# A hybrid recurrent backbone: the modulation product in four column groups, and its weight slots at other places

## The chip, the cores and the metric

The kernel runs on one core of one Trainium2 chip. It is one program with five instruction streams: TensorE (matrix products, PE in the profile), VectorE (DVE), ScalarE (ACT), GpSimd (POOL) and SyncE (SP), which issues the loads of the weights. The metric is the device time of one execution in microseconds, here the median of three.

## The reference

Two layers over 512 positions (256 of context, 256 of latents) with 1024 features. Each layer takes a modulation vector of 6 x 1024 numbers for the context and one for the latents, from a product of SiLU of a condition vector with the matrix ada_w:

```
h   = adaLN(RMSNorm(x))          shift and scale from SiLU(c) (latents) and SiLU(c_ctx) (context)
P   = h W_in
Y_1 = RWKV-7 mixing, Y_2 = retention, Y_3 = HGRN2
x  += gate1 * ( sum_b sigmoid(P_gate_b) * (Y_b W_branch_b) ) W_out
x  += gate2 * SquaredReLU-MLP(adaLN(RMSNorm(x)))
'ada_w': (L, D, 6 * D) = (2, 1024, 6144),  'ada_b': (2, 6144)
```

For the change only the first line matters: 6144 columns for each of two layers, each a sum over 1024 rows, for two condition vectors, so a product with a left side of two columns. Shift and scale of the first norm are needed at the start of a layer, gate1 and the second norm's pair before the output projection and the MLP, gate2 in the MLP.

## The kernel before

All data lie transposed, features on the 128 partitions. The weights come from memory in slots of up to 2.3 MB into a ring of three places (RING = 3). The list of slots (schedule_slots) is also the order in which TensorE uses them. SyncE walks this list: the load of slot i waits until the last product that reads slot i - 3 is finished, since both have the same place in the ring. So three slots at most are in the chip at one time, and a slot that is put into the list takes a place of the ring from those around it.

The matrix ada_w is cut into 24 slots of 512 columns (12 for each layer), called (l, a). ADA_AT says at which place of the program each is used; a function modulation(place) stands at these places in the streams of TensorE, ScalarE and VectorE. For a slot TensorE makes eight products (L435), one for each 128 rows, with a stationary part of two columns, and adds them in one bank of PSUM, on two partitions. Each fp32 product is two instructions in the trace. ScalarE copies the two rows to work (L1455). Later TensorE turns the rows of an earlier slot into columns with four small products (L445), and VectorE adds the bias (L983). The program calls the four small products "ada columns".

Around these places TensorE runs strictly in the order in which the program is written, and so does each other engine. The stages of a layer: a norm (L416 sums squares, ScalarE makes the scaled tiles at L1439, and the first projections wait for them tile by tile), retention (ret_order, four heads), three small projections and then four heads of RWKV-7 (c = 0 to 3; L379 projects, then a long chain of 64x64 products from L401 on), HGRN2 (L736), the gated merge, the output projection (L805), a second norm and the MLP. Place names: "start", "norm1", "strips" (retention), "small" (after the small projections), "kk" and "keys" (in head c of RWKV-7, after its three projections), "out" (end of HGRN2), "norm2", "mlp".

The MLP of layer 0 has 16 slots of weights, mlp_slots. For each slot, a stage, TensorE makes 4 groups of 24 products (L826 to L828 or L840 to L842). Here fp32 values are split in a high and a low part: during stage n ScalarE makes the high part of the weights of slot n + 1 (weights_high, L1402, two halves) and VectorE subtracts it (weights_low, L942, two halves). On VectorE this stands ahead of the four drains of stage n (L1357 or L898):

```
for n, (kind, _, a) in enumerate(mlp_slots(l) ...):
    if n < 15:
        weights_low(l, n + 1)
    for j in range(4):
        ... drain group j of stage n ...
    if n == 1:
        modulation("mlp", l)
```

The results of TensorE's groups go to two banks (big), so group 2 of a stage can only start when VectorE has drained group 0.

## Time and profile before

| | |
|---|---|
| Median of three runs | 2955.51 us (2950.54 to 2956.82) |
| Profiled execution, its span | 2950.0 us |
| PE busy | 2763.4 us (94%) |
| PEld, weight loads of TensorE, beside PE | 1959.7 us (66%) |
| DVE, ACT, POOL busy | 977.6, 659.3, 449.8 us |
| L435, modulation products | 169.5 us busy, 384 instructions |
| L445, rows to columns | 24.0 us busy, 192 instructions |
| Moved by DMA | 239.42 MB, 81 GB/s on average |

The span goes from the first to the last instruction of one profiled execution; its own time is known as this span, and it lies at the low end of the three runs. A row of the timeline has start, duration, engine, line, operation, tiles, count, and in brackets how long the engine was idle before it and what ended that. TensorE is busy nearly all the time, but that says nothing on whether a given piece of its work could be left out without a wait of the same size in its place.

### The profile page before, as it was taken

What the parts mean: (1) busy time and instruction counts of PE and PEld (TensorE: products, weight loads), DVE (VectorE), ACT (ScalarE), POOL (GpSimd) and SP (SyncE); (2) the same over time, 40 slices, a digit from 0 to 9 for tenths busy, and PEclk for the clock granted to TensorE, in tenths of its full rate; (3) what the DMA queues carried; (4) which work ended last, traced back from release to release, by engine and by line L of the source; (5) the groups of instructions that cost most, each with busy time, mean ns of one, the idle gap of its engine ahead of it and who ended that gap; (6) DMA issues with size and microseconds to landing.
All of it is one profiled execution on the core that took longest, in us unless ns stands there. A gap on an engine that the chain in (4) does not pass through costs nothing. (4 is left out here: it accounts for less than half of the span.)

```text
span 2950.0 us, 51713 instructions
## 1 busy us (share of the span) xinstructions
PE 2763.4 (94%) x22928; PEld 1959.7 (66%) x22928; DVE 977.6 (33%) x1594; ACT 659.3 (22%) x923; POOL 449.8 (15%) x567
## 2 busy tenths in 40 slices
PE   8999999999999899999999999999888998799998
PEld 2553847658449656646888757386685657688887
DVE  1323443544116422225444332345444215211000
ACT  3213122331120311122222241323323120301100
POOL 0002221312006400000000000313223107100100
PEclk9999999999996799999999999999998996899999
DMA  7312220201110012232222251201000030143441
GB/s 300 139 50 77 78 80 3 80 5 57 49 70 33 33 64 97 73 126 87 86 101 99 86 194 72 95 25 52 19 14 30 2 121 33 61 157 115 160 154 72
DMA packets 18222, 239.42 MB, mean 81 GB/s; under 512 B 2001, under 2 KB 3153, under 8 KB 3409
## 3 DMA queue, kind: packets, MB, share of 16 engines
q1 hardware_dynamic: 16128, 218.11, 19.7%
q10 hardware_dynamic: 1872, 18.02, 1.5%
q8 instruction: 181, 2.97, 0.4%
q14 instruction: 41, 0.33, 0.0%
HBM read 230.88 MB, written 5.24 MB: 80 GB/s over the span
## 5 line engine op out<-in xcount | busy, mean ns | idle before, releaser
L379 PE MATMUL psum<-normed,weight_ring 128*128 128x256 f32 (+1 forms) x2320 | 771.6, 492 | 32.5 <-DVE work L892 11.5
L379 PEld LDWEIGHTS psum<-normed,weight_ring 128*128 128x128 f32 x2320 | 449.3, 195 | 342.8 <-issue 274.5
L392 PE MATMUL psum<-work 64*64 64x64 f32 (+1 forms) x9088 | 307.7, 222 | 13.9 <-ACT work L1614 10.5
L392 PEld LDWEIGHTS psum<-work 64*64 64x64 f32 x9088 | 294.9, 135 | 25.4 <-issue 14.5
L435 PE MATMUL psum<-weight_ring,derived 128*2 128x512 f32 x384 | 169.5, 602 | 12.4 <-ACT derived L1460 9.6
L898 DVE SCALAR_TENSOR_TENSOR work<-psum,derived,work 128x256 f32<-128x256 f32 x96 | 46.4, 484 | 394.7 <-PE psum L859 218.7
L736 PE MATMUL psum<-work 128*128 128x64 f32 x672 | 139.6, 399 | 13.9 <-DVE work L1277 10.8
L736 PEld LDWEIGHTS psum<-work 128*128 128x128 f32 x672 | 135.3, 310 | 18.0 <-DVE work L1277 12.3
L1204 DVE TENSOR_TENSOR work<-work,psum 128x512 f32<-128x512 f32 x144 | 99.0, 688 | 142.0 <-PE psum L392 141.9
L1778 POOL TENSOR_TENSOR work<-work,constants 128x512 f32<-128x512 f32 x80 | 108.2, 1352 | 205.8 <-DVE work L1187 140.6
L794 PE MATMUL psum<-work,weight_ring 128*128 128x512 f32 (+1 forms) x384 | 131.6, 485 | 0.0
L1801 POOL TENSOR_TENSOR work<-work 128x256 f32<-128x256 f32 x128 | 90.9, 710 | 260.7 <-PE psum L736 251.9
L435 PEld LDWEIGHTS psum<-weight_ring,derived 128*2 128x2 f32 x384 | 30.7, 85 | 141.2 <-issue 127.7
L1722 POOL TENSOR_TENSOR work<-work 128x512 f32<-128x512 f32 (+1 forms) x8 | 6.6, 826 | 746.7 <-DVE work L1069 746.7
L1323 DVE TENSOR_TENSOR work<-psum,work 128x512 f32<-128x512 f32 (+1 forms) x48 | 26.8, 558 | 274.4 <-PE psum L794 229.0
L859 PE MATMUL psum<-work,weight_ring 128*128 128x256 f32 x512 | 111.5, 379 | 0.0
L826 PE MATMUL psum<-normed_high,weights_high 128*128 128x512 f32 x256 | 104.5, 408 | 6.2 <-DVE work L1357 4.4
L859 PEld LDWEIGHTS psum<-work,weight_ring 128*128 128x128 f32 x512 | 97.3, 190 | 13.2
L828 PE MATMUL psum<-normed_high,weight_ring_parts 128*128 128x512 f32 x256 | 103.3, 404 | 0.0
L827 PE MATMUL psum<-normed_low_part,weights_high 128*128 128x512 f32 x256 | 102.8, 402 | 0.0
L840 PE MATMUL psum<-hidden_high,weights_high 128*128 128x512 f32 x256 | 101.8, 398 | 0.0
L842 PE MATMUL psum<-hidden_high,weight_ring_parts 128*128 128x512 f32 x256 | 101.7, 397 | 0.0
(229 smaller groups left out, 3929.8 us busy)
## 6 DMA issues: line engine op xcount, KB each, us to landing
weight_ring<-in_weights SPq DMA_DIRECT2D x78, 2048.0 KB, 7.9
weight_ring<-in_weights SPq DMA_DIRECT2D x16, 2304.0 KB, 8.6
weight_ring<-in_weights SPq DMA_DIRECT2D x10, 1536.0 KB, 6.6
x_scratch<-work ACTq DMA_DIRECT2D x2, 2048.0 KB, 11.5
work<-x_scratch ACTq DMA_DIRECT2D x2, 2048.0 KB, 9.0
work<-in_ret_constants ACTq DMA_DIRECT2D x2, 1152.0 KB, 14.5
work<-in_small_weights ACTq DMA_DIRECT2D x2, 1152.0 KB, 5.2
work<-in_x ACTq DMA_DIRECT2D x1, 2048.0 KB, 26.1
```

The lines of the kernel that those rows point to most:

```text
L379: last = mm(ps[:, 0:t1 - t0], tiled(s, j, k), hT[:, k, t0:t1], start=(k == 0), stop=(k == KT - 1))
L392: last = mm(ps[q, w * m:w * m + w], lhs(q, m), rhs(q, m), start=True, stop=True)
L435: last = mm(ps[rows_at(what), :], der[:, D_CS + 2 * k:D_CS + 2 * k + 2], s[:, BW * k:BW * k + BW], start=(k == 0), stop=(k == KT - 1))
L736: last = mm(cols(ps), k_[dd][:, t], cols(q_[dd]), start=True, stop=True)
L794: last = mm(ps[:, 0:t1 - t0], s[:, w0:w0 + P], work[:, Y[b] + 512 * k + t0:Y[b] + 512 * k + t1], start=(k == 0), stop=(k == NT - 1))
L826: mm(ps, w_hi, hi, start=(k == 0), stop=False)
L827: mm(ps, w_hi, hT_r[:, k, :], start=False, stop=False)
L828: last = mm(ps, s[:, P * t:P * t + P], hi, start=False, stop=(k == KT - 1))
L840: mm(ps, w_hi, hi, start=(k == 0), stop=False)
L842: last = mm(ps, s[:, P * t:P * t + P], hi, start=False, stop=(k == KT - 1))
L859: last = mm(ps[:, 0:t1 - t0], s[:, P * k:P * k + P], work[:, hid(k) + t0:hid(k) + t1], start=(k == 0), stop=(k == 31))
L1778: tt(chunks(B + (KTI if j % 2 else BT)), chunks(B + LT), over_chunks(kcol(K_LEV + 64 * j, 64), 64), ALU.mult).then_inc(pool_rwkv.sem, pool ...
```

## The change

Each slot's eight products now go to four column groups of TensorE's array in turn: the stationary part is 32 columns wide (two of them the condition, the rest zeros, in a new tile cond), and product k writes partitions 32 (k mod 4) to 32 (k mod 4) + 31. ScalarE copies all 128 rows. The four small products then use a matrix of two columns, K_SEL, which adds the four partial sums as they turn rows into columns. There is now one place in work for the rows instead of two, so "ada columns" of a slot follows directly after the products of the next slot, and ScalarE's copy waits for it.

The 24 slots move. Before, the slots of layer 1 were spread over RWKV-7 of layer 0, the end of HGRN2, the norms, and layer 1. Now layer 0's twelve stand at start, strips, small and RWKV-7 of layer 0; ten of layer 1's stand in the MLP of layer 0, one after each of the stages n = 1 to 10; two stand in norm1 and strips of layer 1. None is left at norm1 of layer 0, out, norm2, and small and RWKV-7 of layer 1. The masks of the scan also lose their second half (K_SCAN), the reversed one being equal to the first.

```
@@ -103,13 +104,14 @@
 
 ADA_AT = {
-    ("start", 0): [(0, 0), (0, 1), (0, 2), (0, 3), None], ("norm1", 0): [(0, 4), (0, 5)], ("strips", 0): [(0, 6)],
-    ("small", 0): [(0, 7)],
-    ("kk", 0, 0): [(0, 8)], ("keys", 0, 0): [(1, 0)], ("kk", 0, 1): [(0, 9)], ("keys", 0, 1): [(1, 1)],
-    ("kk", 0, 2): [(0, 10)], ("keys", 0, 2): [(1, 2)], ("kk", 0, 3): [(1, 3)],
-    ("out", 0): [(0, 11)], ("norm2", 0): [(1, 4)], ("mlp", 0): [(1, 5)],
-    ("norm1", 1): [(1, 6), (1, 7)], ("strips", 1): [(1, 8)], ("small", 1): [(1, 9)],
-    ("kk", 1, 0): [(1, 10)], ("kk", 1, 1): [(1, 11)], ("kk", 1, 2): [None],
+    ("start", 0): [(0, 0), (0, 1), (0, 2), (0, 3), None], ("strips", 0): [(0, 4)],
+    ("small", 0): [(0, 5)],
+    ("kk", 0, 0): [(0, 6)], ("keys", 0, 0): [(0, 7)], ("kk", 0, 1): [(0, 8)], ("keys", 0, 1): [(0, 9)],
+    ("kk", 0, 2): [(0, 10)], ("keys", 0, 2): [(0, 11)], ("kk", 0, 3): [None],
+    ("mlp", 0, 1): [(1, 0)], ("mlp", 0, 2): [(1, 1)], ("mlp", 0, 3): [(1, 2)], ("mlp", 0, 4): [(1, 3)],
+    ("mlp", 0, 5): [(1, 4)], ("mlp", 0, 6): [(1, 5)], ("mlp", 0, 7): [(1, 6)], ("mlp", 0, 8): [(1, 7)],
+    ("mlp", 0, 9): [(1, 8)], ("mlp", 0, 10): [(1, 9)], ("mlp", 0, 11): [None],
+    ("norm1", 1): [(1, 10)], ("strips", 1): [(1, 11), None],
 }
 
@@ -149,8 +151,7 @@
         if l < L - 1:
             for n, key in enumerate(mlp_slots(l)):
                 out += [(key, 4 * KT * P)]
-                if n == 1:
-                    ada("mlp", l)
+                ada("mlp", l, n)
         else:
             out += [(("m1", l, a), 4 * KT * P) for a in range(8)]
             out += [(("m2", l, f), 32 * P) for f in range(8)]
@@
+        cond = sb("condition_columns", [P, KT * 32])
@@ -332,14 +334,7 @@
             if what is None:
                 return [rows.pop(0) for _ in range(len(rows))]
             rows.append(what)
-            return [rows.pop(0)] if len(rows) > 2 else []
-
-        ada_order = [what for place in ADA_AT.values() for what in place if what is not None]
-
-        def rows_at(what):
-
-            p0 = 32 + 32 * (ada_order.index(what) % 2)
-            return slice(p0, p0 + 2)
+            return [rows.pop(0)] if len(rows) > 1 else []
 
         ret_order = [("P", 0), ("R", 0), ("P", 1), ("A", 0), ("R", 1), ("O", 0), ("P", 2), ("A", 1), ("N", 0), ("R", 2),
@@ -432,18 +427,17 @@
                         ps = mid.fill("ada", *what)
                         eng.wait_ge(*mid.freed())
                         for k in range(KT):
-                            last = mm(ps[rows_at(what), :], der[:, D_CS + 2 * k:D_CS + 2 * k + 2], s[:, BW * k:BW * k + BW],
-                                      start=(k == 0), stop=(k == KT - 1))
+                            g = 32 * (k % 4)
+                            last = mm(ps[g:g + 32, :], cond[:, 32 * k:32 * k + 32], s[:, BW * k:BW * k + BW],
+                                      start=(k < 4), stop=(k >= 4))
                         last.then_inc(mid_filled.sem, mid_filled.step(("ada", *what)))
                     for before in finished:
-                        q = rows_at(before)
                         eng.wait_ge(loaded_constants.sem, loaded_constants.at("constants"))
                         eng.wait_ge(act_cond.sem, act_cond.at("drained", "ada", *before))
                         ps = outb.fill("ada columns", *before)
                         eng.wait_ge(*outb.freed())
                         for j in range(4):
-                            last = mm(ps[:, 2 * j:2 * j + 2], work[q, ROWS2 + P * j:ROWS2 + P * j + P],
-                                      kc[q, K_ID + q.start:K_ID + q.stop], start=True, stop=True)
+                            last = mm(ps[:, 2 * j:2 * j + 2], wk(ROWS2 + P * j, P), kcol(K_SEL, 2), start=True, stop=True)
                         last.then_inc(out_filled.sem, out_filled.step(("ada columns", *before)))
             eng.wait_ge(loaded_vectors.sem, loaded_vectors.at("vectors"))
@@
-                    if n == 1:
-                        modulation("mlp", l)
+                    modulation("mlp", l, n)
@@
+            nc.vector.memset(cond[:, :], 0.0).then_inc(vec_cond.sem, vec_cond.step(("columns clear",)))
+            eng.wait_ge(vec_cond.sem, vec_cond.n)
@@
-                        G, sg, msk = wk(RW_D[d] + LT), wk(RW_D[d] + WW), kcol(K_SCAN + 512 * d, N)
+                        G, sg, msk = wk(RW_D[d] + LT), wk(RW_D[d] + WW), kcol(K_SCAN, N)
-                            G, sg, msk = G[:, ::-1], sg[:, ::-1], msk[:, ::-1]
+                            G, sg = G[:, ::-1], sg[:, ::-1]
@@ -1447,17 +1441,18 @@
                 for what in ADA_AT.get(place, ()):
                     if what is not None:
-                        q = rows_at(what)
                         eng.wait_ge(mid_filled.sem, mid_filled.at("ada", *what))
-                        if len(rows) > 1:
-                            eng.wait_ge(out_filled.sem, out_filled.at("ada columns", *rows[-2]))
+                        if rows:
+                            eng.wait_ge(out_filled.sem, out_filled.at("ada columns", *rows[-1]))
                         rows.append(what)
-                        act(work[q, ROWS2:ROWS2 + BW], mid.get("ada", *what)[q, :], ACT.Copy).then_inc(
+                        act(wk(ROWS2), mid.get("ada", *what), ACT.Copy).then_inc(
                             act_cond.sem, act_cond.step(("drained", "ada", *what)))
                         eng.wait_ge(act_cond.sem, act_cond.n)
             eng.wait_ge(loaded_vectors.sem, loaded_vectors.at("vectors"))
-            act(dcol(D_CS, 16), par[:, L * NPL + 8:L * NPL + 24], ACT.Silu).then_inc(act_cond.sem, act_cond.step(("cond silu",)))
+            eng.wait_ge(vec_cond.sem, vec_cond.at("columns clear"))
+            act(cond.rearrange("p (k m) -> p k m", m=32)[:, :, 0:2],
+                par[:, L * NPL + 8:L * NPL + 24].rearrange("p (k s) -> p k s", s=2), ACT.Silu).then_inc(act_cond.sem, act_cond.step(("cond silu",)))
             eng.wait_ge(act_cond.sem, act_cond.n)
             eng.wait_ge(vec_cond.sem, vec_cond.at("lb centred"))
             act(dcol(D_TMP + 8, 16), dcol(D_TMP + 8, 16), ACT.Exp).then_inc(act_cond.sem, act_cond.step(("lb exp",)))
@@
-    k[:, K_SCAN:K_SCAN + N], k[:, K_SCAN + N:K_SCAN + 2 * N] = t % C != 0, t % C != C - 1
+    k[:, K_SCAN:K_SCAN + N] = t % C != 0
+    k[:, K_SEL], k[:, K_SEL + 1] = p % 32 == 0, p % 32 == 1

```

At two places TensorE's order shows the move. The first is the MLP of layer 0 behind its stages 1 and 2; weights_high_0 and _1 are the high parts of the slots, L826 to L828 and L840 to L842 are L820 to L822 and L834 to L836 of the changed kernel. Before:

```order
1480 L828 MATMUL psum<-normed_high,weight_ring_parts 128x512
1481 L435 MATMUL psum<-weight_ring,derived 2x512 x8
1482 L445 MATMUL psum<-constants,work 128x2 x4
1483 L840 MATMUL psum<-hidden_high,weights_high_0_58 128x512
...
1578 L842 MATMUL psum<-hidden_high,weight_ring_parts 128x512
1579 L840 MATMUL psum<-hidden_high,weights_high_0_60 128x512
```

The same places in the changed kernel:

```order
1474 L822 MATMUL psum<-normed_high,weight_ring_parts 128x512
1475 L431 MATMUL psum<-weight_ring,condition_columns 32x512 x8
1476 L834 MATMUL psum<-hidden_high,weights_high_0_58 128x512
...
1571 L836 MATMUL psum<-hidden_high,weight_ring_parts 128x512
1572 L431 MATMUL psum<-weight_ring,condition_columns 32x512 x8
1573 L440 MATMUL psum<-constants,work 128x2 x4
1574 L834 MATMUL psum<-hidden_high,weights_high_0_60 128x512
```

Before, one slot's products stood behind stage 1 and none between stage 2 and stage 3; now there is one behind each of stages 1 to 10, and with it one slot in the ring between each two MLP slots.

The second is the end of that MLP and the start of layer 1: the last sums of squares, the first projections (L379, now L374) and the products of the values (L474, now L468). Before:

```order
2832 L416 MATMUL psum<-work,constants 128x512 x3
2833 L435 MATMUL psum<-weight_ring,derived 2x512 x8
2834 L445 MATMUL psum<-constants,work 128x2 x4
2835 L435 MATMUL psum<-weight_ring,derived 2x512 x8
2836 L445 MATMUL psum<-constants,work 128x2 x4
2837 L379 MATMUL psum<-normed,weight_ring 128x256 x8
2838 L379 MATMUL psum<-normed,weight_ring 128x512 x8
2839 L435 MATMUL psum<-weight_ring,derived 2x512 x8
2840 L445 MATMUL psum<-constants,work 128x2 x4
2841 L474 MATMUL psum<-weight_ring,normed 128x128 x32
```

And in the changed kernel:

```order
2844 L411 MATMUL psum<-work,constants 128x512 x3
2845 L431 MATMUL psum<-weight_ring,condition_columns 32x512 x8
2846 L374 MATMUL psum<-normed,weight_ring 128x256 x8
2847 L374 MATMUL psum<-normed,weight_ring 128x512 x8
2848 L431 MATMUL psum<-weight_ring,condition_columns 32x512 x8
2849 L440 MATMUL psum<-constants,work 128x2 x8
2850 L468 MATMUL psum<-weight_ring,normed 128x128 x32
```

One slot's products instead of two stand between the norm and the first projection that waits for it.

## Rows read from the trace of the kernel before

**Rows 1.** Groups by line and shape, TensorE: the modulation products.
```profile
L435 PE MATMUL psum<-weight_ring,derived 128*2 128x512 f32 x384 | 169.5, 602 | 12.4 <-ACT derived L1460 9.6 <-DMA weight_ring<-in_weights 2.8
```

**Rows 2.** Timeline of TensorE, RWKV-7 of layer 0, head 0: start, us, what.
```profile
285.88 7.13 PE L379 MATMUL psum<-normed,weight_ring 128*128 128x512 f32 x16 [0.57 <-ACT work L1526]
292.94 7.03 PE L435 MATMUL psum<-weight_ring,derived 128*2 128x512 f32 x16
299.90 1.05 PE L445 MATMUL psum<-constants,work 2*128 2x2 f32 x8
...
378.68 1.98 PE L385 MATMUL psum<-work,constants 128*128 128x512 f32 x4 [1.10 <-DVE work L1231]
```

**Rows 3.** Timeline of TensorE, products of two 64x64 quarters in turn.
```profile
432.08 1.96 PE L401 MATMUL psum<-work 64*64 64x128 f32 x32
```

**Rows 4.** Start of the program: a window (DMA share, GB/s last), TensorE's timeline.
```profile
10.00:28.00 18.00, 15.24 (x33) 2.72 (x32) 1.40 (x8) 2.86 (x5) 0.00 (x0) 0.98 1.01 430
...
27.61 8.53 PE L435 MATMUL psum<-weight_ring,derived 128*2 128x512 f32 x16 [2.76 <-DMA weight_ring<-in_weights]
...
46.81 9.21 PE L416 MATMUL psum<-work,constants 128*128 128x512 f32 x16
```

**Rows 5.** Timelines at the first norm of layers 0 and 1.
```profile
68.06 14.00 PE L379 MATMUL psum<-normed,weight_ring 128*128 128x512 f32 x32
...
60.93 10.10 ACT L1439 ACTIVATE normed<-work,derived 128x256 f32<-128x256 f32 x16 [0.91 <-DVE work L919]
...
1723.21 10.59 PE L379 MATMUL psum<-normed,weight_ring 128*128 128x256 f32 x32
...
1712.33 10.10 ACT L1439 ACTIVATE normed<-work,derived 128x256 f32<-128x256 f32 x16 [0.91 <-DVE work L919]
```

**Rows 6.** Timelines of layer 1, before and at its first RWKV-7 head.
```profile
1889.47 4.09 PE L536 MATMUL psum<-work 64*128 64x512 f32 x8
...
1879.00 0.42 ACT L1544 ACTIVATE work<-work 128x256 f32<-128x256 f32 x1
```

**Rows 7.** Timeline of TensorE, RWKV-7 of layer 0, head 3.
```profile
654.43 7.13 PE L379 MATMUL psum<-normed,weight_ring 128*128 128x512 f32 x16
...
677.27 3.68 PE L401 MATMUL psum<-work 64*64 64x128 f32 x32 [4.01 <-DVE work L1178]
...
744.58 1.98 PE L385 MATMUL psum<-work,constants 128*128 128x512 f32 x4 [1.09 <-DVE work L1231]
```

**Rows 8.** Timeline of TensorE, RWKV-7 of layer 1, heads 1 and 2.
```profile
2014.04 7.13 PE L379 MATMUL psum<-normed,weight_ring 128*128 128x512 f32 x16 [0.80 <-ACT work L1526]
...
2101.15 1.13 PE L385 MATMUL psum<-work,constants 128*128 128x256 f32 x4 [0.58 <-DVE work L1231]
...
2126.87 7.13 PE L379 MATMUL psum<-normed,weight_ring 128*128 128x512 f32 x16 [0.88 <-ACT work L1526]
...
2213.80 1.13 PE L385 MATMUL psum<-work,constants 128*128 128x256 f32 x4 [0.58 <-DVE work L1231]
```

**Rows 9.** Timeline of TensorE, end of HGRN2 and second norm of layer 0.
```profile
1021.76 0.70 PE L385 MATMUL psum<-work,constants 128*128 128x512 f32 x1 [1.63 <-POOL work L1814]
...
1322.52 0.47 PE L826 MATMUL psum<-normed_high,weights_high 128*128 128x512 f32 x1 [0.42 <-DVE normed_low_part L932]
```

**Rows 10.** Windows and timelines of the MLP of layer 0, stages 1 to 3.
```profile
1367.40:1381.00 13.60, 13.56 (x49) 10.62 (x50) 5.54 (x8) 1.89 (x3) 0.00 (x0) 0.83 0.00 0
1389.00:1411.20 22.20, 22.20 (x97) 18.04 (x98) 7.65 (x9) 4.44 (x3) 0.00 (x0) 1.00 0.23 90
...
L1842 SPq DMA_DIRECT2D weight_ring<-in_weights x5: 327/328/328, 1351.9 to 1433.5; - x5
...
1359.99 3.87 ACT L1402 ACTIVATE weights_high<-weight_ring 128x2048 fp32r<-128x2048 f32 x2 [5.87 <-DMA weight_ring<-in_weights]
...
1362.04 4.62 DVE L942 TENSOR_TENSOR weight_ring_parts<-weight_ring,weights_high 128x2048 fp32r<-128x2048 f32 x2 [7.13 <-ACT weights_high L1402]
...
1367.44 0.79 PE L826 MATMUL psum<-normed_high,weights_high 128*128 128x512 f32 x1 [4.44 <-DVE work L1357]
```

More of the change, by code:

```diff
@@ L53 @@
 K_SCAN = 2048
-K_EPS = 3072
-K_ID2 = 3076
-NCONST = 3140
+K_EPS = 2560
+K_ID2 = 2564
+K_SEL = 2628
+NCONST = 2630
 R_COS, R_SIN, R_LAG = 0, 512, 1024
@@ L67 @@
 NPAR = L * NPL + 8 + 16
-D_MOD, D_HMU, D_QMU, D_OMU, D_OMKA, D_WS1, D_WS2, D_LG, D_CS, D_LOW, D_OML = (
-    0, 96, 111, 126, 141, 145, 161, 177, 185, 201, 217)
-D_TMP = 233
-NDER = 265
+D_MOD, D_HMU, D_QMU, D_OMU, D_OMKA, D_WS1, D_WS2, D_LG, D_LOW, D_OML = (
+    0, 96, 111, 126, 141, 145, 161, 177, 185, 201)
+D_TMP = 217
+NDER = 249
 Y = [0, 2048, 4096]
@@ L1370, in _ @@
                                 vec_mlp.also(("drained", "m2", l, f))
-                    if n == 1:
-                        modulation("mlp", l)
+                    modulation("mlp", l, n)
                 for f in range(KT if l == L - 1 else 0):
@@ L1701, in _ @@
                         eng.wait_ge(act_mlp.sem, act_mlp.n)
-                    if n_ == 1:
-                        modulation("mlp", l)
+                    modulation("mlp", l, n_)
                 for f in range(32 if l == L - 1 else 0):
```

## The prediction, made blind

> **What bounds the kernel now.** I read the page's table of engines first: PE is busy 94% of the span, so the order of TensorE's work sets the time, and the reader is to see which pieces of that work hide a wait. Then the groups by line: L435 is 384 instructions for 24 slots, 16 a slot, 169.5 us in all, 7.06 us a slot [rows 1]; with the four small products a slot costs 7.03 + 1.05 less their overlap, 8.0 us [rows 2]. If all of it were bare TensorE time, the 24 slots would be 193 us. Then the timelines around each place, to see what comes behind the product, and last the MLP of layer 0, where the new slots go: which load does a VectorE instruction wait for, and who waits for VectorE.
>
> **T, the price of one slot's products.** The trace has no product in several column groups with all rows in use. The nearest row has two quarters of the array, in turn: 32 products of 128 columns in 1.96 us, of which some 0.2 is the last one's tail, so 0.055 us each [rows 3]. One such instruction by itself would take 7.03/16 x 128/512 = 0.11 us [rows 2]. So two run at once there, and I see no more than two in any row. Bounds: 7.0 us (nothing runs at once) and 7.0/4, with a tail 1.9 us. Each product is two instructions for one group, the second of which can't pass the first; if starts are in order, then in the row g0, g0, g1, g1, ... the second half of one group runs beside the first half of the next, and never more. That is 9 steps of 0.44 us for 16 instructions: T = 4.0 us. It is also what halving by rows 3 gives (3.5) with a step to begin and end. I take 4.0. With its small products a slot is then 5.0 us, against 8.0.
>
> The Trainium skill (TensorE: Matmul & The Clock Gate, Part 3: Packing small matmuls) states that matmuls start and end strictly in program order, and a measured 2.38x for three column tiles of 512 columns; by the latter the products would take 7.0/2.38 = 3.0 us or less, an estimate that lies between my T and the lower bound. No row here shows four column groups. The in-order rule is the one that speaks against the full factor of four, and rows 3 agree with it so far as they go.
>
> **The slots outside the MLP, place by place.**
> Start of layer 0: four slots. The DMA moves 430 GB/s from 10 to 28 us [rows 4], its most in the trace, so the third slot lands at 27.6 us whatever TensorE does; a slot of 2.1 MB is 4.9 us at that rate, so the fourth lands at 32.5. Third product: 5.4 us at the low clock that follows the wait (the row's 8.53 against 7.03 shows such a clock), to 33; small ones to 34; fourth to 38; its copy must now wait for the small products before it, so the last small ones end at 40.7. Before, the norm began at 46.8 [rows 4]: gain 6.
> First norm of both layers: two slots stood there. ScalarE's tiles take 10.10 us and end at 71.0 and 1722.4; the projections began at 68.1 and 1723.2 [rows 5]. TensorE will now wait for tiles and go by them: the first projection ends 3 and 3.7 us sooner. The wait lowers the clock for a few us, so I take 5 for both instead of 6.8.
> strips and small of layer 0: 8.0 becomes 5.0 each, gain 6 for both. strips of layer 1 also gets one more set of small products: gain 2. small of layer 1 goes: gain 8, since what comes behind it, L536 at 1889.5, needs ScalarE's result of 1879.4 and so has 10 us to spare [rows 6].
> RWKV-7 of layer 0: two slots in heads 0 to 2, one in head 3. From the third projection to the sums at the end head 0 takes 92.8 us [rows 2], head 3 with one slot less takes 90.2 [rows 7]: 8.0 us of products taken away give 2.65, the rest turns into the 4.0 us wait for VectorE at L1178 and a slower L401 behind it [rows 7]. Two slots at T = 4.0 make 10 us, near head 3's 8: gain 2.65 x 3 = 8. Head 3 loses its slot: gain 0, it waits already.
> RWKV-7 of layer 1: head 1 with a slot takes 87.1 us, head 2 with two sets of small products (2 us) 86.9 [rows 8]. The slots were cover for a wait: gain 0 for both.
> out: the sums behind it wait for POOL anyway [rows 9]: gain 1. norm2: the MLP's first product comes at 1322.5 and waits for the split of its input by VectorE [rows 9], not for the slot: gain 0, and 8 us of idle TensorE ahead of it, -1 for the clock.
> Clearing cond, the scan's mask and 128 rows instead of 2 in ScalarE's copy (the same 512 columns) cost nothing: VectorE clears while TensorE waits for its first data.
> Sum: 6 + 5 + 6 + 2 + 8 + 8 + 0 + 1 - 1 = 35 us gained. With T = 1.9: 9 + 5 + 10 + 4 + 8 + 8 + 0 + 1 - 1 = 44.
>
> **The MLP of layer 0.** A stage at full speed is 96 products in 22.2 us, 5.55 a group [rows 10]. Stage 1 shows what a slot in the ring does. The load of MLP slot 2 had to wait for the end of stage 0 and was issued at 1351.9 [rows 10]; ScalarE had it at 1360.0, 8.1 us later; VectorE could begin L942 after the first half, at 1362.0, needed 4.62, and only then drained group 0; TensorE, done with groups 0 and 1 at 1363.0, waited 4.4 us until 1367.4, then did the last two groups at granted clock 0.83 in 13.6 us instead of 11.1 [rows 10]. Behind VectorE's L942 stand all drains of the stage, behind these the banks, behind these TensorE. Stage 1 was 29 us instead of 22.2. Stage 2, with its load issued earlier, ran at 22.2 [rows 10].
> In the changed kernel this is the rule. MLP slot n + 1 takes the place of modulation slot n - 1, whose products end about 1 us before stage n; ahead of it on the queue stands modulation slot n, released at the end of stage n - 1, T earlier. Counted from the end of stage n - 1: the modulation slot lands at 8.0, the MLP slot 4.9 later, 12.9 (its own issue at T = 4.0 plus 8 is sooner, so the rate decides). Then as in stage 1: 2.0 for ScalarE's first half, 4.6 for L942, 0.7 for the drain: group 2 starts at 20.2. TensorE was ready at 4.0 + 1.05 + 11.1 = 16.1, so it waits 4.1 us. With 11.1 for two groups the period is 31.3 us, plus 2.5 where the clock falls as in stage 1; I take half of that: 32.5. This holds for n = 2 to 10, nine times: 9 x (32.5 - 22.2) = 93. Stage 11 adds one slot without a stall (5.0) and one set of small ones (1.05); before's slot in the MLP goes (-8.0). Sum: 91 us lost. Bounds: without any fall of the clock 80, with one each time 102. T hardly matters here, since the load sets the period.
>
> **The sum.** 91 - 35 = +56 us on a span of 2950.0. The median of the runs, 2955.5, lies 5.5 above this span; so 3012 us, slower by 1.9%.
>
> **Rivals.**
> All four groups at once: T = 1.9. The period in the MLP stays 32.5, stage 11 costs 3 us less: 89 - 44 = +45, 3001 us. For it: nothing in the change limits it to two. Against: rows 3.
> The groups don't run at once: T = 7.0. Then the MLP slot is issued at 7 and lands at 15, period 34.6, loss 112 + 1; outside the MLP only what stood free counts, 2 + 5 + 8 + 1 - 1 - 1 = 14: +99, 3055 us. For it: here all groups read the same rows, in rows 3 each quarter has its own.
> The loads come in time: the MLP slot lands by 8.8 us (16.1 less the 7.3 behind it), and stages stay at 22.2. Then the MLP costs 10 x 5.0 - 8.0 + 1.05 - 1.05 = 42, and 42 - 35 = +7, 2962 us; with T = 1.9 it would be 21 - 44 = -23. For it: the DMA is idle half of each stage. Against: stage 1, where even a single load came 4.4 us late.
> On the other side, faster: outside the MLP TensorE is the bound everywhere, as 94% says, and whatever leaves it comes off the time. Before, 23 slots at 8.0 stood outside, now 14 at 5.0: 184 - 70 = 114 us gained against 91, -23, 2932 us. It decides from 91 us of gain on, 2.6 times my sum. Against: rows 7 and 8, where 8 us less gave 2.65 and 0.2.
>
> **How the numbers follow.** Forecast 0.45, T = 1.9 0.24, no concurrency 0.12, loads in time 0.11, TensorE the bound 0.08. The forecast's own spread is the clock (+-11) and a few us for each place. The time is the forecast's, 3012. The range reaches down past the case of 3001 with no fall of the clock (2990) and part of the way to loads that land early, 2972, and up to half way to the case of 3055, 3040. A difference under 0.2% (6 us) can't be told from none. Slower by more: the first three cases and half of the fourth, 0.86. Within: 0.04. Faster: 0.10.
>
> **What would show it.** L431's 384 instructions: a slot in 4.0 us, or 1.9, or 7.0. In the MLP of layer 0 TensorE waits some 4 us for L1352's drain or the add behind weights_low in each of stages 2 to 10, weights_high waits for the DMA, and the stretch from the first MLP product to the first norm of layer 1 is some 90 us longer; if the waits are missing, the forecast is wrong. In RWKV-7 of layer 1 nothing gets shorter; in layer 0 heads 0 to 2 get shorter by some 3 us each, with a new wait for L1178. SyncE's queue in the MLP waits for L431.

## The result and the profile after: slower by 2.4%

The changed kernel takes 3021.66 us, median of four runs (3020.16 to 3026.92), against 2953.03 (2949.03 to 2956.82) for four runs of the kernel before: ratio 1.0241, interval 1.0224 to 1.0258. The profiled executions have spans of 3018.8 and 2950.0 us, so the account below is of +68.8 us. One execution of a later kernel, the spread places, was in a slower state (3159.8 us at a granted clock of 0.811, its other four at 0.933 to 0.938) and is left out of every number.

From the page of the changed kernel, first its table of engines, then three groups by line (busy us, mean ns | idle before, and on what):

```profile
PE 2691.1 (89%) x22928; PEld 1965.7 (65%) x22928; DVE 978.2 (32%) x1595; ACT 659.0 (22%) x923; POOL 449.3 (15%) x567
```

```profile
L431 PE MATMUL psum<-weight_ring,condition_columns 128*32 128x512 f32 x384 | 51.3, 656 | 18.5 <-ACT condition_columns L1454 9.5 <-DMA weight_ring<-in_weights 9.0
L440 PE MATMUL psum<-constants,work 128*128 128x2 f32 x192 | 26.4, 260 | 11.9 <-issue 11.9
...
L935 DVE TENSOR_TENSOR weight_ring_parts<-weight_ring,weights_high 128x2048 fp32r<-128x2048 f32 x32 | 73.4, 2292 | 130.8 <-ACT weights_high L1396 130.2
```

The products fell from 169.5 us of busy time [rows 1] to 51.3. PE is busy 72.3 us less than before, and the span is 68.8 us longer: TensorE idles 141 us more. In the trace of before VectorE's L942 (here L935) has 25.4 us of idle time ahead of it; now 130.8 stand there. The waits of TensorE (what it waited for: us in all, times, longest) say the same from its side:

```profile
PE psum L396 <- DVE work L1173: 49.5, 8, 8.7
PE psum L834 <- DVE work L891: 38.1, 6, 7.7
PE psum L820 <- DVE work L1352: 32.7, 5, 7.3
```

In the kernel before, RWKV-7 waited less, and the drains of the MLP made TensorE wait once, 4.4 us:

```profile
PE psum L401 <- DVE work L1178: 20.9, 5, 6.6
...
PE psum L826 <- DVE work L1357: 4.4, 1, 4.4
```

Eleven waits, 70.8 us, are now in the MLP of layer 0 (L834, L820), one in each of the stages 1 to 11. The first row is RWKV-7: 28.6 us more than before, as slots that were cover for it are gone or shorter: with slots of 7.05 us in the same places (the run of the places alone, below) it is 32.9 us in five waits, and heads 0 to 2 of layer 0, which keep two slots each, have none of them.

The timeline of TensorE from the start to the second projection (start, us, engine, line):

```profile
9.50 3.64 PE L431 MATMUL psum<-weight_ring,condition_columns 128*32 128x512 f32 x16 [9.50 <-ACT condition_columns L1454]
...
31.80 1.92 PE L431 MATMUL psum<-weight_ring,condition_columns 128*32 128x512 f32 x16
...
36.41 7.68 PE L411 MATMUL psum<-work,constants 128*128 128x512 f32 x16
50.38 16.79 PE L374 MATMUL psum<-normed,weight_ring 128*128 128x512 f32 x32 [6.29 <-ACT normed L1433]
67.10 1.93 PE L431 MATMUL psum<-weight_ring,condition_columns 128*32 128x512 f32 x16
```

A slot's 16 instructions take 1.92 us, and 3.64 behind a wait. The norm begins 10.4 us sooner than in [rows 4], and the first projection ends 15.0 us sooner than in [rows 5].

Now the MLP, TensorE from the slot behind stage 1 to that behind stage 10, and the chain on ScalarE and VectorE that it waits for:

```profile
1343.73 1.93 PE L431 MATMUL psum<-weight_ring,condition_columns 128*32 128x512 f32 x16
...
1377.94 1.92 PE L431 MATMUL psum<-weight_ring,condition_columns 128*32 128x512 f32 x16
...
1399.88 0.80 PE L834 MATMUL psum<-hidden_high,weights_high 128*128 128x512 f32 x1 [7.74 <-DVE work L891]
...
1412.86 1.92 PE L431 MATMUL psum<-weight_ring,condition_columns 128*32 128x512 f32 x16
...
1434.34 0.79 PE L820 MATMUL psum<-normed_high,weights_high 128*128 128x512 f32 x1 [7.32 <-DVE work L1352]
...
1447.14 1.92 PE L431 MATMUL psum<-weight_ring,condition_columns 128*32 128x512 f32 x16
...
1651.82 1.92 PE L431 MATMUL psum<-weight_ring,condition_columns 128*32 128x512 f32 x16
```

```profile
1392.13 3.85 ACT L1396 ACTIVATE weights_high<-weight_ring 128x2048 fp32r<-128x2048 f32 x2 [10.57 <-DMA weight_ring<-in_weights]
...
1394.17 4.62 DVE L935 TENSOR_TENSOR weight_ring_parts<-weight_ring,weights_high 128x2048 fp32r<-128x2048 f32 x2 [13.05 <-ACT weights_high L1396]
1398.82 2.04 DVE L891 SCALAR_TENSOR_TENSOR work<-psum,derived,work 128x256 f32<-128x256 f32 x4
```

The nine periods from the first of these rows to the last take 308.1 us, 34.2 each, where stage 2 of before took 22.2 [rows 10]; the two shown are 34.9 and 34.3. Counted from 1377.94: the load is there at 14.2, L935 starts at 16.2, TensorE goes on at 21.9, having been ready at 14.2 too. Behind the wait the granted clock is lower, as a window over the last two groups of a stage shows (us, busy of five engines, granted clock, DMA share, GB/s):

```profile
1364.30:1377.90 13.60, 13.59 (x48) 10.61 (x48) 1.93 (x4) 0.00 (x0) 0.00 (x0) 0.82 0.00 0
1399.90:1412.80 12.90, 12.90 (x48) 10.16 (x48) 1.90 (x4) 0.00 (x0) 0.00 (x0) 0.86 0.00 0
```

11.1 us of products take 13.6 and 12.9, as in stage 1 of before [rows 10].

### The profile page after: what moved, and what is told of

The parts are those of the page before. It is cut to its first block and busy times, and to the rows that moved or that the text cites. A ratio compares the mean times of both kernels' runs of the same rounds, so it can differ in the third digit from the quotient of the medians.

```text
span 3018.8 us, 51716 instructions
## 1 busy us (share of the span) xinstructions
PE 2691.1 (89%) x22928; PEld 1965.7 (65%) x22928; DVE 978.2 (32%) x1595; ACT 659.0 (22%) x923; POOL 449.3 (15%) x567
## 5 line engine op out<-in xcount | busy, mean ns | idle before, releaser
L374 PE MATMUL psum<-normed,weight_ring 128*128 128x256 f32 (+1 forms) x2320 | 783.1, 497 | 41.7 <-ACT normed L1433 15.7
L374 PEld LDWEIGHTS psum<-normed,weight_ring 128*128 128x128 f32 x2320 | 453.3, 197 | 361.6 <-issue 287.0
L387 PE MATMUL psum<-work 64*64 64x64 f32 (+1 forms) x9088 | 307.3, 223 | 12.5 <-ACT work L1609 10.2
L387 PEld LDWEIGHTS psum<-work 64*64 64x64 f32 x9088 | 294.3, 135 | 24.0 <-issue 12.4
L820 PE MATMUL psum<-normed_high,weights_high 128*128 128x512 f32 x256 | 108.4, 424 | 41.8 <-DVE work L1352 32.7
L834 PE MATMUL psum<-hidden_high,weights_high 128*128 128x512 f32 x256 | 108.2, 423 | 38.1 <-DVE work L891 38.1
L396 PE MATMUL psum<-work 64*64 64x128 f32 (+1 forms) x1024 | 73.3, 308 | 65.3 <-DVE work L1173 49.5
L1318 DVE TENSOR_TENSOR work<-psum,work 128x512 f32<-128x512 f32 (+1 forms) x48 | 26.8, 558 | 274.8 <-PE psum L788 228.8
L935 DVE TENSOR_TENSOR weight_ring_parts<-weight_ring,weights_high 128x2048 fp32r<-128x2048 f32 x32 | 73.4, 2292 | 130.8 <-ACT weights_high L1396 130.2
L396 PEld LDWEIGHTS psum<-work 64*64 64x64 f32 x1024 | 64.6, 167 | 70.7 <-DVE work L1173 50.6
L835 PE MATMUL psum<-hidden_low,weights_high 128*128 128x512 f32 x256 | 105.3, 411 | 0.0
## 6 DMA issues: line engine op xcount, KB each, us to landing
work<-in_x ACTq DMA_DIRECT2D x1, 2048.0 KB, 25.4
```

Of the source, the lines that this page charges most:

```text
L374: last = mm(ps[:, 0:t1 - t0], tiled(s, j, k), hT[:, k, t0:t1], start=(k == 0), stop=(k == KT - 1))
L387: last = mm(ps[q, w * m:w * m + w], lhs(q, m), rhs(q, m), start=True, stop=True)
L396: last = mm(ps[q, 128 * m:128 * m + n], lhs(q, m), work[q, B + KR + 128 * m:B + KR + 128 * m + n], start=True, stop=True)
L820: mm(ps, w_hi, hi, start=(k == 0), stop=False)
L834: mm(ps, w_hi, hi, start=(k == 0), stop=False)
L835: mm(ps, w_hi, hidden_lo[:, k, :], start=False, stop=False)
```

## Experiments

All ratios are to the kernel before, timed beside it on the same chip; the chips differ from one group of experiments to the next, so medians of different groups are compared only roughly.

**Does the order of the groups matter?** The products of a column group were put next to each other (0, 0, 32, 32, 64, ...) instead of in turn. If an instruction can start only when the one before it has, four instructions in a row for one group stand in the way of the next group.

```
-                            g = 32 * (k % 4)
+                            g = 32 * (k // 2)
-                                      start=(k < 4), stop=(k >= 4))
+                                      start=(k % 2 == 0), stop=(k % 2 == 1))
```

> The changed kernel, but two products in a row go to the same column group (0, 0, 1, 1, 2, 2, 3, 3) instead of 0, 1, 2, 3, 0, 1, 2, 3. Theory Q (each column group has its own order, and a later group passes an earlier one that waits): a slot's products still take 1.9 us and the time stays at 3022. Rival O (starts are in program order, and an instruction waits for its group's predecessor): 13 steps of 0.43, 5.7 us a slot, and 3035 to 3050 us.

Measured: 3018.51 us (3014.01 to 3027.87), ratio 1.0228 [1.0208, 1.0248], the same as the changed kernel. One slot in its timeline:

```profile
241.95 1.94 PE L431 MATMUL psum<-weight_ring,condition_columns 128*32 128x512 f32 x16
```

1.94 us against 1.92. The four groups run beside each other in either order, where starts in program order would have given 5.7 us, by the count in the expectation. So the in-order start that gave my T = 4.0 doesn't hold here; that each column group keeps an order of its own is what fits both times, but the trace doesn't name the group of an instruction. The Trainium skill (TensorE: Matmul & The Clock Gate, Part 3: Packing small matmuls) states that matmuls start and end strictly in program order; by it this kernel would have needed well over 1.94 us a slot, and this measurement does not agree with it for products in different column groups.

**The groups alone, and the places alone.** One kernel has the four groups, two row places in work, and the places of before; only the three slots from small of layer 1 on went to places just behind the first projections of the retention heads of layer 1. Its stationary part is 32 neighbouring columns of a narrower cond; thirty of them give sums that nobody reads. The other has the new places, with all products in one column group (g = 0, 32 rows copied).

```
+                            g = 32 * (k % 4)
+                            last = mm(ps[g:g + 32, :], cond[:, 2 * k:2 * k + 32], s[:, BW * k:BW * k + BW],
+                                      start=(k < 4), stop=(k >= 4))
...
-    ("norm1", 1): [(1, 6), (1, 7)], ("strips", 1): [(1, 8)], ("small", 1): [(1, 9)],
-    ("kk", 1, 0): [(1, 10)], ("kk", 1, 1): [(1, 11)], ("kk", 1, 2): [None],
+    ("norm1", 1): [(1, 6), (1, 7)], ("strips", 1): [(1, 8)], ("ret", 1, 1): [(1, 9)],
+    ("ret", 1, 2): [(1, 10)], ("ret", 1, 3): [(1, 11), None],
```

> The four column groups with the slots where they stood before (places of rows doubled so that two slots can stand in a row; the last three slots of layer 1, whose row space collides with other data now, stand behind the projections of retention heads 1 to 3 instead). Theory R (the move of ten slots into the MLP costs the time, since each takes a ring place and its MLP neighbour's load starts a stage late, and VectorE's split of the weights stands ahead of its drains): the MLP keeps one stall as before and the groups' gain shows: about 2914 us, 39 under the kernel before. Rival G (the grouped product itself slows what is around it): 2950 or more.

> The changed kernel's places, but all eight products of a slot in one column group, one after the other, 7.0 us a slot. Theory R: the stall in the MLP is set by the load, so the slower product adds only some 2 us to each of nine stages, about 10 at the start and 15 to 20 elsewhere: about 3070 us. Rival P (TensorE's own time is what counts everywhere): 24 x 5.1 us more, 3144 us.

Measured: groups alone 2917.04 us (2914.58 to 2923.4), ratio 0.9891 [0.9872, 0.991]; places alone 3070.06 (3068.61 to 3072.48), ratio 1.0403 [1.0388, 1.0419]. So the two halves of the change have opposite signs: -33 and +120. They add up to +87, not to the +69 of both, since the groups save 33 us in the old places and 48 in the new. The one place for rows instead of two goes with the places here; it was never changed by itself. Places alone, TensorE at the first product of the MLP, then behind stages 1 to 3 and 10:

```profile
1314.27 0.77 PE L820 MATMUL psum<-normed_high,weights_high 128*128 128x512 f32 x1 [8.36 <-DVE normed_low_part L925]
...
1371.31 7.05 PE L431 MATMUL psum<-weight_ring,condition_columns 128*32 128x512 f32 x16
...
1408.20 7.05 PE L431 MATMUL psum<-weight_ring,condition_columns 128*32 128x512 f32 x16
...
1430.87 0.79 PE L834 MATMUL psum<-hidden_high,weights_high 128*128 128x512 f32 x1 [3.25 <-DVE work L891]
...
1443.80 7.05 PE L431 MATMUL psum<-weight_ring,condition_columns 128*32 128x512 f32 x16
...
1694.92 7.05 PE L431 MATMUL psum<-weight_ring,condition_columns 128*32 128x512 f32 x16
```

The nine periods average 36.0 us with products of 7.05 us, against 34.2 with 1.92: T is 5.1 us longer, the period 1.8. In the stage from 1408.20 the load is there at 14.9 instead of 14.2, and TensorE goes on at 22.7 instead of 21.9, after a wait of 3.25 instead of 7.74 us. So the load sets most of the period; of T a third comes through, as the MLP slot's own load is issued only behind these products. Ahead of the MLP T counts for more: its first product comes at 1314.27 here and at 1286.33 in the changed kernel, 27.9 us for the 5.1 of T.

**Is it the order of VectorE's work, or the load itself?** In the first kernel the split of the next slot's weights is moved behind the drains that it stood ahead of (VectorE's L935 to behind the second of the four drains, ScalarE's L1396 beside it in the stages of the first kind); all loads stay. In the second the ten slots of the MLP are not loaded and have no place in the ring; their products read v_first, so layer 1's modulation is not computed in it. With three MLP slots in the ring, each one's load is then issued a whole stage sooner.

```
-                    if n < 15:
-                        weights_low(l, n + 1)
...
+                        if j == 2 and n < 15:
+                            weights_low(l, n + 1)
```

> The changed kernel, but in each MLP stage VectorE and ScalarE make the next slot's weights after the first two groups are drained, not before. Theory R: the late load hides behind the first two groups' drains, each of nine stages falls from 34.0 to about 25.2 us: about 2942 us. Rival D (the loads themselves, by traffic or by the weights being late for the stage after): the stages stay at 30 or more, 3000 to 3022 us.

> The changed kernel, but the ten slots in the MLP are neither loaded nor given a place in the ring; their products run on other data that lie in the chip (the modulation of layer 1 is not computed). TensorE's work is the same. Theory R: stages fall from 34.0 to 25.2 us, about 2942 us. Rival P (TensorE's products or the clock after them make the stages long): 3010 to 3022 us.

Measured: drains first 2934.23 us (2931.22 to 2936.72), ratio 0.9942 [0.9926, 0.9957]; no loads 2929.91 (2927.75 to 2935.14), ratio 0.993 [0.9913, 0.9947]. Either takes away the whole MLP loss, 87 and 92 us, and in neither trace does TensorE wait for a drain of the MLP. Both gained more than I had expected, by 8 and 12: the nine stages are worth 9 x 9.0 = 81 us, and I had not counted the wait of stage 1 (4.31 us in the changed kernel, with a lower clock behind it), which goes too. Drains first, TensorE and then the two groups that make the split:

```profile
1391.39 1.92 PE L431 MATMUL psum<-weight_ring,condition_columns 128*32 128x512 f32 x16
...
1441.86 1.92 PE L431 MATMUL psum<-weight_ring,condition_columns 128*32 128x512 f32 x16
```

```profile
L1396 ACT ACTIVATE weights_high<-weight_ring 128x2048 fp32r<-128x2048 f32 x32 | 61.4, 1918 | 54.4 <-DMA weight_ring<-in_weights 53.6
...
L935 DVE TENSOR_TENSOR weight_ring_parts<-weight_ring,weights_high 128x2048 fp32r<-128x2048 f32 x32 | 73.3, 2292 | 12.8 <-ACT weights_high L1396 12.1
```

Two periods take 50.5 us, 25.2 each: 22.2 of the stage and 3.0 of the slot. ScalarE still waits 53.6 us for the loads, and they are nearly as late as in the changed kernel: the MLP slot's load landed 13.6 us behind the start of the products (issued at 1393.4, 11.6 us to land), against 14.1 there. But TensorE no longer waits for it. The late load costs only because the split stands ahead of the drains in VectorE's order. Both conditions are needed: take away either and the cost is gone.

**The wait at strips of layer 1.** TensorE, changed kernel:

```profile
1801.17 1.92 PE L431 MATMUL psum<-weight_ring,condition_columns 128*32 128x512 f32 x16
...
1815.14 1.84 PE L440 MATMUL psum<-constants,work 128*128 128x2 f32 x8 [11.06 <-issue]
1816.84 8.81 PE L468 MATMUL psum<-weight_ring,normed 128*128 128x128 f32 x64
```

and ScalarE, whose copy L1448 the last set of small products waits for:

```profile
1804.08 0.61 ACT L1489 ACTIVATE work<-work,derived 128x384 f32<-128x384 f32 x1 [2.15 <-DMA work<-in_ret_constants]
...
1813.79 0.62 ACT L1495 ACTIVATE work<-work,derived 128x384 f32<-128x384 f32 x1
1814.44 0.60 ACT L1448 ACTIVATE work<-psum 128x512 f32<-128x512 f32 x1
```

The copy stands behind 16 exponentials, 10.3 us of ScalarE's time, the first of which waits 2.15 us for constants to land. To test it, the last set of small products alone was moved to behind the first projections of the second retention head.

```
-    ("norm1", 1): [(1, 10)], ("strips", 1): [(1, 11), None],
+    ("norm1", 1): [(1, 10)], ("strips", 1): [(1, 11)], ("ret", 1, 1): [None],
```

> The changed kernel, but the last slot's small products in layer 1 stand behind the projections of retention head 1 instead of directly behind its products at strips. Theory W (TensorE waits 11 us there, since ScalarE's copy of the rows stands behind its sixteen exponentials, which wait for constants from memory): the wait goes and about 9 us with it, 3013 us. Rival (the time is needed anyway by the retention behind it): 3020 to 3022 us.

Measured: 3010.7 us (3006.26 to 3013.9), ratio 1.0206 [1.0189, 1.0223]. TensorE's idle time ahead of the small products, put down to its own issue, fell from 11.9 us (L440 above) to 0.8. The medians differ by 11 us, the profiled pair by 6.7. But the pair were apart before the place of the change: the sums that end the MLP come at 1776.9 us here and at 1773.2 in the changed kernel, whose orders are the same up to there. From there to the end this kernel is 10.3 us shorter, which agrees with the medians: the wait was worth about 10 us.

**Towards a better kernel.** The groups alone, with the split behind the drains:

> The grouped product with the slots where they stood before (as in the run of the groups alone, 2917 us), and the weights of the next MLP slot made after the first two groups are drained. Theory R: the one stall that the kernel before had in stage 1 of the MLP (6.8 us) goes: about 2910 us. Rival: the later split delays the stages after it, 2917 us or more.

Measured: 2907.05 us (2904.06 to 2912.56), ratio 0.9858 [0.984, 0.9875]. The order of the drains pays some 10 us even with the places of before.

All slots behind the start in the RWKV-7 heads, three to a head in layer 0 and two in layer 1, on the ground that a wait for VectorE or ScalarE hides them there; the split stays ahead of the drains, and no slot stands in the MLP:

```
+    ("kk", 0, 0): [(0, 4), (0, 5), (0, 6)], ("kk", 0, 1): [(0, 7), (0, 8), (0, 9)],
+    ("kk", 0, 2): [(0, 10), (0, 11), (1, 0)], ("kk", 0, 3): [(1, 1), (1, 2), (1, 3), None],
+    ("kk", 1, 0): [(1, 4), (1, 5)], ("kk", 1, 1): [(1, 6), (1, 7)],
+    ("kk", 1, 2): [(1, 8), (1, 9)], ("kk", 1, 3): [(1, 10), (1, 11), None],
```

> The grouped product, with all slots but the first four in the RWKV-7 heads, three in each head of layer 0 and two in each of layer 1, behind the third projection, where TensorE waits for VectorE anyway; none in the MLP, the norms or retention (the rows have a place of their own). Theory C (only the places with a wait are free, and three slots of 3 us with one late load fit in front of the 15.8 us that VectorE needs): about 2890 us. Rival: three loads in a row come too late for the head or its successor, 2915 us or more.

Measured: 2914.03 us (2911.34 to 2917.03), ratio 0.9879 [0.9864, 0.9895]: 24 us worse than the theory. TensorE's waits in it:

```profile
PE psum L437 <- issue: 29.4, 6, 7.4
PE psum L428 <- DMA weight_ring<-in_weights: 18.7, 7, 4.3
...
PE psum L437 <- DVE derived L975: 10.7, 3, 4.6
```

Of the 18.7 us for loads 8.4 are at the start, as in the changed kernel; the rest is in the heads. Head 1 of layer 1 takes 90.6 us from its third projection to the sums with two slots (1965.84 to 2056.44), against 87.1 with one in the kernel before [rows 8]. A slot alone in its place is cheap; several in one place wait for each other's load, for ScalarE's copy and for the one place for rows. So the next kernel spread them: the split behind the drains, one row place, the places one by one.

```
+    ("out", 0): [(1, 1)], ("norm2", 0): [(1, 2)], ("mlp", 0, 1): [(1, 3)], ("mlp", 0, 3): [None],
+    ("norm1", 1): [(1, 4)], ("strips", 1): [(1, 5)], ("ret", 1, 1): [(1, 6)], ("ret", 1, 2): [(1, 7)],
+    ("kk", 1, 0): [(1, 8)], ("kk", 1, 1): [(1, 9)], ("kk", 1, 2): [(1, 10)], ("kk", 1, 3): [(1, 11), None],
```

> The modulation product in four column groups, the copies that split the weights placed ahead of the drains, and the places spread one by one: one slot of ten in each head of layer 1's RWKV, where one slot stood free of cost before (rows 8), and only two kept in the MLP of layer 0. Theory (a slot is free wherever it stands alone and its split is in time): about 2900 us, 2893 to 2907, the products 1.92 us each. Rival (the ring keeps a slot's load late and the next head's projections wait for it, or the split steals time from the drains): 2907 us or more, no better than the grouped places with the early split.

> The same kernel as the grouped places with the early split, run beside the spread places so that the two are compared on one chip: 2907 us, within 5.

The first of these two texts says that the split is placed ahead of the drains and that two slots are kept in the MLP; in the kernel the split stands behind the second drain, and one slot is in the MLP of layer 0.

Measured: 2901.4 us (four executions, 2900.23 to 2902.7), ratio 0.9836 [0.9821, 0.9851]. Beside it the grouped places with the split behind the drains gave 2906.23 (2901.44 to 2911.93), ratio 0.9859 [0.9839, 0.9879]. The intervals overlap; that the spread places are better by some 5 us is likely, not shown. A second time, for its profile:

> The spread places once more, for their profile: 2901 us, within 5. By the theory no stage of the MLP waits longer than stage 1 did before (4.4 us), and TensorE waits for a slot's load or its split nowhere in layer 1's RWKV; by the rival those waits show there.

Measured: 2903.81 us (2902.27 to 2904.85), ratio 0.9837 [0.982, 0.9853]. No wait for a drain is left in the MLP. But in each head of layer 1 TensorE waits for ScalarE's copy of the slot's rows: 5.4, 6.8 and 6.8 us in heads 0 to 2, ahead of L387. These cost next to nothing: head 1 takes 87.4 us from its third projection to the sums (1961.99 to 2049.37), against 87.1 before [rows 8]. In head 3 the wait for the copy of slot (1,11) is longer:

```profile
2187.30 7.13 PE L374 MATMUL psum<-normed,weight_ring 128*128 128x512 f32 x16 [0.62 <-ACT work L1526]
...
2207.56 1.83 PE L440 MATMUL psum<-constants,work 128*128 128x2 f32 x8 [9.24 <-issue]
...
2221.11 1.54 PE L396 MATMUL psum<-work 64*64 64x64 f32 x32
```

Is that wait worth something? Each layer 1 slot one place earlier, so that (1,11) stands in head 2 and only its small products in head 3:

> As the spread places, but the layer 1 slots each one place earlier: a third slot in the MLP of layer 0, (1,11) in head 2 and only its small products in head 3 of layer 1's RWKV, where the spread places had TensorE wait 9.2 us for ScalarE's copy with nothing between. Theory (the wait costs what it shows, less what the head hides anyway; the slot in the MLP costs its 3 us): 2898 us, 2893 to 2901. Rival (head 3 waits for VectorE anyway, so the 9.2 us were hidden and only the slot's 3 us are added): 2905 to 2908.

Measured: 2905.79 us (2896.46 to 2905.98), ratio 0.9841 [0.982, 0.9861]: the rival's number, though the intervals of the two kernels overlap. The same head:

```profile
2193.94 7.13 PE L374 MATMUL psum<-normed,weight_ring 128*128 128x512 f32 x16 [0.88 <-ACT work L1526]
...
2217.27 2.82 PE L396 MATMUL psum<-work 64*64 64x64 f32 x32 [6.53 <-DVE work L1177]
...
2224.74 1.54 PE L396 MATMUL psum<-work 64*64 64x64 f32 x32
```

From the third projection to the last L396 group it is 33.8 us with the wait of 9.24 and 30.8 without: 6.5 us of the wait came back as a wait for VectorE. The 3 us gained were paid for the second slot in the MLP (the expectation calls it the third): from the MLP's first product to its last sums this trace is 3 us longer. The spread places, at 2901 to 2904 us, have the lowest medians of all, 1.6% under the kernel before.

## Why the prediction was right, and which of its terms were not

The sign, the place and the mechanism held; the time was 10 us short, and that it was no more is in part luck, since errors of both signs met in it. The account by rows, from one point of the program to the next; negative is gained:

| Stretch | Predicted | Measured |
|---|---|---|
| Start, to the norm: 46.81 to 36.41 | -6 | -10.4 |
| To the end of the first projection: 82.06 to 67.10 | -2.5 | -4.6 |
| strips and small of layer 0, to head 0's third projection: 285.88 to 260.63 | -6 | -10.3 |
| Layer 0 heads 0 to 2, to head 3's third projection: 654.43 to 618.96 | -8 | -10.2 |
| Head 3, out, norm2, to the MLP's first product: 1322.52 to 1286.33 | 0 | -0.7 |
| MLP and first norm of layer 1, to the slot at strips: 1733.73 to 1801.17 | +88.5 | +103.6 |
| Slot at strips, to L468 (before L474): 1741.67 to 1816.84 | -2 | +7.7 |
| Rest of layer 1, to the end | -8 | -6.4 |
| Sum | +56 | +68.8 |

Each measured number is how much the shift between the two kernels changes over the stretch; the times are starts, 82.06 is the end 68.06 + 14.00 [rows 5], and the last stretch runs to the ends of the spans. Other points of before are in [rows 2, 4, 7, 9]. Those that the groups of before don't show are these, before's TensorE and then the changed kernel's:

```profile
1733.73 7.03 PE L435 MATMUL psum<-weight_ring,derived 128*2 128x512 f32 x16
...
1741.67 7.41 PE L474 MATMUL psum<-weight_ring,normed 128*128 128x128 f32 x64
```

```profile
260.63 7.13 PE L374 MATMUL psum<-normed,weight_ring 128*128 128x512 f32 x16 [0.56 <-ACT work L1521]
...
350.77 1.98 PE L380 MATMUL psum<-work,constants 128*128 128x512 f32 x4 [1.22 <-DVE work L1226]
...
618.96 7.13 PE L374 MATMUL psum<-normed,weight_ring 128*128 128x512 f32 x16
...
1286.33 0.77 PE L820 MATMUL psum<-normed_high,weights_high 128*128 128x512 f32 x1 [8.36 <-DVE normed_low_part L925]
```

- **T = 4.0 us: wrong, 1.92.** It rested on an in-order start, and the pairs of the same group (1.94 us) refute that. The term had been taken at twice its size; the rival at 0.24 had it right. The rows used for halving [rows 3] can't have shown the limit of four groups: they had two quarters. With T = 1.9 the prediction gave 9 and 10 for the first and third row of the table, which is most of the first and the whole of the third.
- **First norm: mis-sized.** TensorE goes by ScalarE's tiles until 59.1 us, and its granted clock is 0.50 from 50 to 54 us, 0.86 from 54 to 58 and 1.00 after that: 16.79 us for what took 14.00 [rows 5]. The wait ahead is 6.29; still 4.6 gained against 2.5.
- **RWKV-7 of layer 0: right.** Head 0 takes 90.1 us from the third projection to the sums, 2.7 less than in [rows 2], as the 2.65 of the step. Its two slots give up 2 x 5.1 us of products, and a wait of 6.00 us for L1173 and a slower L396 behind it (3.68 us against 1.96 in [rows 3]) take most of it back:

```profile
283.67 3.68 PE L396 MATMUL psum<-work 64*64 64x128 f32 x32 [6.00 <-DVE work L1173]
```

  Heads 0 to 2 together gave 10.2 rather than 8.
- **Layer 1's RWKV-7, out and norm2: right.** Next to nothing was gained there (head 1 without its slot takes 86.7 us, 2083.16 to 2169.84, against 87.1 [rows 8]); before the MLP's first product TensorE now waits 8.36 us, the 8 of the step.
- **The MLP: mechanism right, size short.** The period is 34.2 us where I had 32.5. In the stage read above the load is there at 14.2 where I had 12.9, TensorE is released 7.7 behind it against 7.3, at 21.9 instead of 20.2; and the clock takes 1.8 to 2.5 us where I took half of 2.5. 9 x 1.7 = 15 us, the excess of the row. TensorE waits some 7 us a stage instead of 4, as it is ready 1.9 us sooner (14.2 instead of 16.1) and released 1.7 later. That T matters little there is shown by the places alone, 36.0 on average with T = 7.05, where the prediction had 34.6.
- **strips of layer 1: wrong.** I counted one more set of small products there and a gain of 2. I did not look at what stands in front of ScalarE's copy in its own order: 16 exponentials and their constants, 11.06 us of wait for TensorE, and a lower clock behind it (8.81 us for L468, 7.41 before), which is also 1.4 of the 1.6 us that the last row of the table is short.
- **Net.** The places ahead of the MLP gave 13.7 us more than forecast, mostly by T: by the places alone, 5.1 us of T are worth 27.9 us there, so the 2.1 between 4.0 and 1.92 are worth some 11, an estimate in proportion; the MLP lost 15.1 more, strips of layer 1 9.7 more, the rest of layer 1 gave 1.6 less. That leaves 12.8 on a forecast of +56; the medians differ by the same 68.6. One slip in the rivals: for T = 1.9 stage 11 costs 2 us less, not 3; the 89 goes by 2.

What stays open: what the one place for rows costs by itself; and whether the spread places beat the grouped ones, which would take more runs.

## What to carry to other kernels

Before you add work between the stages of a pipeline, look at what its load does to the load that comes behind it in the same ring, and at the place that the consumer of that next load has in its engine's order. A step that prepares the next stage should stand behind the drains that the current stage waits for: a late load then costs nothing (2934 us here instead of 3022). And a piece of TensorE's work that stands in a wait is free only once; two of them in the same wait (90.6 us a head instead of 87.1), or one whose last step hangs on another engine's long queue (about 10 us at strips), are not.

## What the runs showed of the hardware

- Products in four column groups of 32, all 128 rows in use and 512 columns, run four at a time: 1.92 us for 16 instructions, against 7.03 one after another, 3.7 times. The Trainium skill (TensorEngine Tiling (Array Packing), Theoretical Speedup) gives up to 4 as the theoretical factor, and the trace comes near it. The order of the groups makes no difference (1.94 us).
- At half clock the same takes 3.64 us, 1.9 times as long: the third slot, with a granted clock of 0.50 from 26.8 to 30.6 us.
- A lone load of a slot was there 8.1 us after its issue in stage 1 of before [rows 10]. In the changed kernel two stand behind each other, and the eight issued from 1343.8 to 1449.1 us took 7.8 to 12.1 us to land, median 10.0.
